# FoX prompt attention written out step by step, with projections between its steps and the past's bias summed page by page

## What is computed

```python
h = rmsnorm(x, ln_g);  z = h @ w_in          # fq fk fv ff fg | gq gk gv glr gg | ma mb
fq, fk = rmsnorm per head;  logf = log_sigmoid(ff + b)
# prompt: causal softmax(q k^T * scale + c_q - c_k) @ v with c = cumsum(logf)
# sample: the same over 32 paged blocks of 128 past tokens and the 8 new ones
lf_past = cache_logf[page_table];  c_past = cumsum(lf_past over 4096 tokens)
a = (o_fox * silu(fg)) @ w_up_a;  b = (rmsnorm(o_gla) * silu(gg)) @ w_up_b
y = x + (sigmoid(ma) * a + sigmoid(mb) * b) @ w_out
```

## Time and profile before

| | us |
|---|---|
| median of 3 runs | 1828.0 (1827.0 to 1829.68) |
| the profiled execution | 1815.63 |
| its span, first to last instruction | 1813.9 |
| PE / DVE / ACT / POOL busy | 1564.8 / 689.7 / 621.1 / 493.4 |
| mean granted TensorE clock | 0.951 of full |

### The profile page before, as it was taken

The page is one execution under the profiler, slowest core; times in us unless marked ns, Lnnn a source line. Parts: engine busy times, 40 slices in busy tenths (PEclk is TensorE's granted clock), DMA queues, the critical chain, the costliest instruction groups (busy, mean ns, idle before and its releaser), DMA issues. The chain is left out here.

```text
span 1813.9 us, 35678 instructions
## 1 busy us (share of the span) xinstructions
PE 1564.8 (86%) x11525; PEld 1304.4 (72%) x11525; DVE 689.7 (38%) x1513; ACT 621.1 (34%) x1319; POOL 493.4 (27%) x935
## 2 busy tenths in 40 slices
PE   3597979889669898899988999999987748999998
PEld 2494858778458676688766887768755548888887
DVE  5326153442643444534445344453443112333211
ACT  5135242434422434324343244442433225111111
POOL 0042332423262134233332333443140012111000
PEclk7699999999979999999999999999998879999999
DMA  4111212212055376667666666776655542322143
GB/s 130 46 47 25 81 32 60 51 53 59 14 155 168 112 225 213 208 189 211 209 201 205 198 199 203 222 228 192 200 162 165 170 179 93 141 96 85 50 117 113
DMA packets 154692, 249.72 MB, mean 138 GB/s; under 512 B 37321, under 2 KB 63434, under 8 KB 153954
## 3 DMA queue, kind: packets, MB, share of 16 engines
q1 hardware_dynamic: 122978, 215.78, 38.2%
q0 software_dynamic: 31552, 31.96, 6.6%
HBM read 217.40 MB, written 30.22 MB: 137 GB/s over the span
## 5 line engine op out<-in xcount | busy, mean ns | idle before, releaser
L280 PE MATMUL psum<-h_hi,w_hi 128*128 128x384 f32 (+1 forms) x1536 | 555.5, 362 | 62.5 <-issue 31.7
L280 PE MATMUL psum<-h_hi,w_lo 128*128 128x384 f32 (+1 forms) x1536 | 511.8, 333 | 0.0
L280 PE MATMUL psum<-h_lo,w_hi 128*128 128x384 f32 (+1 forms) x1536 | 511.3, 333 | 0.0
L280 PEld LDWEIGHTS psum<-h_hi,w_hi 128*128 128x128 f32 x1536 | 296.7, 193 | 130.2 <-issue 117.0
L1239 POOL DMA_DIRECT2D sc<-tmp_bias x512 | 252.6, 502 | 304.4 <-PE psum L1674 300.6
L280 PEld LDWEIGHTS psum<-h_lo,w_hi 128*128 128x128 f32 x1536 | 297.6, 194 | 3.0
L280 PEld LDWEIGHTS psum<-h_hi,w_lo 128*128 128x128 f32 x1536 | 296.0, 193 | 0.0
L579 POOL DMA_DIRECT2D lfk<-in_cache_logf x256 | 136.9, 535 | 259.1 <-issue 259.1
L1643 PE MATMUL psum<-con,k_page 128*128 128x128 f32 x1024 | 154.6, 277 | 32.8 <-DVE k_t L1168 22.2
L1643 PEld LDWEIGHTS psum<-con,k_page 128*128 128x128 f32 x1024 | 121.9, 142 | 53.8 <-issue 49.2
L1293 ACT ACTIVATE k_t<-psum 128x512 f32<-128x512 f32 x128 | 75.9, 593 | 201.0 <-PE psum L1643 200.8
(11 more groups left out here) (242 smaller groups left out, 2003.1 us busy)
## 6 DMA issues: line engine op xcount, KB each, us to landing
k_page<-in_cache_k SPq DMA_DIRECT2D x256, 256.0 KB, 3.5
v_page<-in_cache_v SPq DMA_DIRECT2D x256, 256.0 KB, 3.1
w_raw<-in_w_tiles SPq DMA_DIRECT2D x64, 512.0 KB, 4.6
g_pair<-tmp_gates SPq DMA_DIRECT2D x16, 544.0 KB, 4.6
sc<-tmp_bias POOLq DMA_DIRECT2D x512, 16.0 KB, 2.9
tmp_gates<-tm POOLq DMA_DIRECT2D x24, 192.0 KB, 3.5
tmp_ogla<-gate POOLq DMA_DIRECT2D x4, 1088.0 KB, 5.9
g_pair<-tmp_ogla SPq DMA_DIRECT2D x8, 544.0 KB, 4.9
```

Source lines behind the costliest of these rows:

```text
L280: m = pe.matmul(out, wt[:, s, k, :], h[:, k, t0:t0 + w], start=(k == 0 and a == 0), stop=(k == KT_ - 1 and a == 2))
```

## The change

1. `build_fox` no longer loops. `fox_order` writes one list of steps that all engines follow: the projections of pair 0 up to the first chunk of its gate tile, then the attention of pair i with the remaining gate chunks of pair i and the projections of pair i+1 between its steps. A chunk is cut into four parts of 6 matmuls. In the last pair two of the 12 merge gates that GLA projected take that place. Parts are placed in proportion to the costs in the list.
2. The ring has two banks, 0 and 1. Banks 6 and 7 take, in turn, everything else that is copied out (`lifted`): transposes, sums of squares, weighted values. A step waits until the one two places before it has been copied. `q_fm`, `k_fm`, `v_tok` and `ofox` get a second buffer.
3. The gate's sigmoid is done straight from the bank, one chunk at a time, without parking.
4. The past: a page of log forgets lands as one row of 4 KB on one partition, 128 pages in each of two groups. DVE scans the 128 tokens of each head in a page (8 scans per group), one matmul with a constant triangle (`later`) sums the later pages, and DVE subtracts. The scans of group 0 stand in DVE's list in pair 1, those of group 1 in pair 2, each after step 30 of the attention (behind t = 3's scores and before query block 1 is gated). SP stores each group in four DMAs.
5. `build_gla` has 34 projection tiles instead of 36.

```diff
-        with pe.Fori(0, NHP) as i:
...
+def projection_steps():
+    out, after = [], {}
+    tiles = fox_tiles()
...
+            if kind in (K, Q):
+                e = 3 * (kind - K) + c
+                later(n, c, FOX_PARTS - 1, (("sq", n, c), 0))
+                later(n, c + 1, 0, (("nm", i, e), 0.65), (("evac", n, c), 0))
+            else:
+                later(n, c + 1, 0, (("evac", n, c), 0))
...
+def attention_steps(i):
+    def scores(t):
+        return [(("sc", i, t), 0.28 * (t + 1) + 0.1)]
+    def soft(t, hh):
+        return [(("sm", i, t, hh), 0), (("ex", i, t, hh), 0)]
+    def turn(t, g):
+        n = min(4, t + 1 - 4 * g)
+        return [(("pt", i, t, g, hh), 0.11 * n + 0.05) for hh in range(2)]
+    out = scores(0) + soft(0, 0) + soft(0, 1)
+    for t in range(TT):
+        more = t + 1 < TT
+        if more:
+            out += scores(t + 1)
+        out += turn(t, 0)
+        if more:
+            out += soft(t + 1, 0)
+        if t >= 4:
+            out += turn(t, 1)
+        if more:
+            out += soft(t + 1, 1)
+        out.append((("inv", i, t), 0))
+        if t:
+            out.append((("pv", i, t - 1), 0.22 * t + 0.3))
...
+    for i in range(NHP):
+        k = cut(("z", 4 * i + G, 1, 0))
+        steps += [s for s, _ in proj[:k]]
+        proj = proj[k:]
+        k = cut(("z", 4 * (i + 1) + G, 0, 0)) if i < NHP - 1 else len(proj)
+        fill, proj = proj[:k], proj[k:]
+        own = attention_steps(i)
+        if i in (1, 2):
+            own = own[:30] + [(("lfscan", i - 1, h), 0) for h in range(H)] + own[30:36] + [(("lf", i - 1), 0.2)] + own[36:]
+        total, work = sum(c for _, c in fill), sum(c for _, c in own)
+        done = placed = 0.0
+        for s, cost in own:
+            steps.append(s)
+            done += cost * total / work
+            while fill and placed + fill[0][1] <= done + 0.3:
+                placed += fill[0][1]
+                steps.append(fill.pop(0)[0])
...
-        stream.phase(0, 4, (6, 0, 1))
+        stream.phase(0, 0, (0, 1))
...
+        def lift_bank(*st):
+            return bank[6 + lift_of[st][0] % 2]
+        def wait_bank(eng, *st):
+            n = lift_of[st][0]
+            if n >= 2:
+                wait_copied(eng, *lift_at[n - 2])
...
-                with pool.Fori(0, NHP) as i:
-                    W(pool, "lf_turned2", i, 2, 0)
-                    for g in range(PG):
-                        for b in range(NB):
-                            page = pool.value_load(pages[0:1, ds(i * PG + (b * NPG + g), 1)], min_val=0, max_val=NPHYS - 1)
-                            pool.dma_start(lfk[:, g, b * H:(b + 1) * H], ins["cache_logf"][ds(page, 1)]
-                                           .rearrange("o p h -> (o p) h")).then_inc(lf_in, 16)
+                for a in range(NB * NPG):
+                    page = pool.value_load(pages[0:1, a:a + 1], min_val=0, max_val=NPHYS - 1)
+                    pool.dma_start(lfp[a % P:a % P + 1, a // P, :], ins["cache_logf"][ds(page, 1)]
+                                   .rearrange("o p h -> o (p h)")).then_inc(lf_in[a // P], 16)
...
+                    if kind == G:
+                        sig = eg[:, 0:w]
+                        sigmoid_dve(dve, lambda name: W(dve, name, i, 3, c + 1), inc, zb, sig)
+                        W(dve, "g_sig", i, 3, c + 1)
...
+                        T(ofox[:, i % 2, t0:t0 + wp], zb[:, 0:wp], sig[:, 0:wp], ALU.mult).then_inc(stream.z_read, 1)
...
-                dve.tensor_tensor_scan(lfc[:], one[0:NB * H, :].to_broadcast([NB * H, PAST]), lfc[:], 0.0, ALU.mult,
-                                       ALU.add).then_inc(past_cum, 1)
...
+                def lf_scan(g, h):
+                    if h == 0:
+                        dve.wait_ge(one_set, 1)
+                        dve.wait_ge(lf_in[g], 16 * P)
+                        if g:
+                            dve.wait_ge(b_stored, 4 * 16)
+                    dve.tensor_tensor_scan(lfc[:, h, :], one[:].to_broadcast([P, PAGE]),
+                                           lfp[:, g, :].rearrange("p (t h) -> p h t", h=H)[:, h, :], 0.0, ALU.mult, ALU.add).then_inc(page_cum, 1)
+                def lf_bias(g):
+                    wait_lifted(dve, "lf", g)
+                    dve.tensor_copy(suffix[:], lift_bank("lf", g)[:, 0:H]).then_inc(lift_dve, 1)
+                    wait_copied(dve, "lf", g)
+                    T(lfc[:], suffix[:].unsqueeze(2).to_broadcast([P, H, PAGE]), lfc[:], ALU.subtract).then_inc(bias_set, 1)
...
+GATES_IN_FOX = 2
-    out, m = [], 2 * KT_ - GATES_AT_END
+    out, m = [], 2 * KT_ - GATES_AT_END - GATES_IN_FOX
-        stream.phase(TT * 2, 0, (0, 1))
+        stream.phase(4 * NHP + GATES_IN_FOX, 0, (0, 1))
```

More of the change, by code:

```diff
@@ L57 @@
 NCONST = _w
+CONST_W["later"] = (_w, 128)
 VEC_W = {}
@@ L482, in _, with fox_tiles @@
                 m.then_inc(lf_turned, 1)
[L485 to L495, removed]
+V, K, Q, G = range(4)
+FOX_PARTS = 4
+FOX_LIFTED = ("vt", "kt", "nm", "pt", "pv", "lf")
+def fox_tiles():
+    return [(n, i) for i in range(NHP) for n in (V, K, Q, G)] + [("m", x) for x in range(GATES_IN_FOX)]
@@ new lines, in projection_steps, with later @@
+def projection_steps():
+    out, after = [], {}
+    tiles = fox_tiles()
+    def later(n, c, part, *steps):
+        at = 3 * n + c
+        after.setdefault((at // 3, at % 3, part), []).extend(steps)
+    for n, (kind, i) in enumerate(tiles):
+        for c in range(3):
+            if kind in (K, Q):
[4 more added lines that the diff above has]
+                later(n, c + 1, 0, (("evac", n, c), 0))
+        for p in range(3):
+            if kind == V:
+                later(n, 3, p + 1, (("vt", i, p), 0.45))
+            if kind == K:
+                later(n, 4, p + 1, (("kt", i, p), 0.45))
+    for n in range(len(tiles)):
+        for c in range(3):
+            for part in range(FOX_PARTS):
+                out.append((("z", n, c, part), 1.05))
+                out += after.pop((n, c, part), [])
+    for key in sorted(after):
+        out += after[key]
+    return out
@@ new lines, in fox_order, with cut @@
+def fox_order():
+    proj = projection_steps()
+    steps = [("cbc", 0)]
+    def cut(step):
+        return next((k for k, (s, _) in enumerate(proj) if s == step), len(proj))
+    for i in range(NHP):
[15 more added lines that the diff above has]
+                steps.append(fill.pop(0)[0])
+        steps += [s for s, _ in fill]
+        steps.append(("end", i))
+    return steps
@@ L569, in _ @@
+                run(sp, {"cbc": bias_rows, "z": z, "vt": v_store, "kt": k_store, "lf": bias_store, "end": end})
+                for s in range(2):
+                    sp.wait_ge(of_stored[s], NHP // 2 * 16)
+                sp.wait_ge(v_stored, NHP * 32)
+                sp.wait_ge(k_stored, NHP * 32)
+                sp.wait_ge(b_stored, 8 * 16)
             @block.gpsimd
@@ new lines, in square @@
+                def square(n, c):
+                    kind, i = tiles[n]
+                    e = 3 * (kind - K) + c
+                    w = CHUNKS[c][1]
+                    act.wait_ge(stream.projected, stream.chunk(0, n, c))
+                    if e >= 2:
+                        wait_lifted(act, "nm", i, e - 2)
+                    elif i:
+                        wait_lifted(act, "nm", i - 1, e + 4)
+                    inc(act.activation(sq[:, e % 2, 0:w], stream.bank_of(n, c), ACT.Square), "squared")
@@ L790, in turn_kv @@
[L790 to L800 removed]
+                opened(pe, lifted, S["s_mm"], S["pv_mm"])
@@ L829, in weigh @@
-                def weigh(i, t):
-                    W(pe, "pt0", i, NG, group(t, t // 4) + 1)
-                    W(pe, "pt1", i, NG, group(t, t // 4) + 1)
-                    W(pe, "o_gated", i, TT, t)
-                    if t == 0:
-                        pe.wait_ge(stream.z_read, stream.chunk(i, G, 2))
+                        for hh, head in enumerate(heads):
+                            m = pe.matmul(bank[2 + 2 * hh + c // 4][:, 0:n], q_fm[head, i % 2, t * P:(t + 1) * P],
+                                          k_fm[head, i % 2, c * P:c * P + n], start=True, stop=True)
@@ L896 @@
+                run(pe, {"z": z, "vt": v_turn, "kt": k_turn, "nm": norm_sum, "sc": scores, "pt": turn_prob, "pv": weigh, "lf": page_suffix})
 PARTS = 4
```

563 lines of the change are left out of this document (267 added, 296 removed).

## The result

| | before | after |
|---|---|---|
| median of 20 runs of each, us | 1822.33 | 1834.82 |
| ratio, 95% interval | | 1.0058, 1.0042 to 1.0075 |
| the profiled execution, its span | 1815.6, 1813.9 | 1832.1, 1830.4 |
| first matmul of GLA | 515.56 | 558.46 |
| first matmul of the merge | 1476.4 | 1492.88 |

The change makes the kernel slower by 0.6%. 1860 was predicted, within 1800 to 1880: the direction came out, but the loss was 12.5 us by the medians where 32 were forecast. By stages, in the two traces: FoX ends 42.9 us later, GLA takes 26.4 us less, and the merge is the same, +16.5 us.

A forecast was written before the change was run, and what follows sets the result against it. PE was taken as the bound, with idle time in FoX's attention and end; a 52 us page wait starts GLA 52 us later, less 20 in GLA is +32 us, put on the median: 1860, range 1800 to 1880.

The forecast's parts named there:

- PE released from the page wait: FoX, third pair: PE idles 52 us, from 358 to 410, while DVE waits for pages until 405, then scans and gates.
- from there to FoX's last matmul: FoX after the page wait: 131 us of list, 2.5 us for the low clock, 1 + 13 us of waits.
- to GLA's first: End of FoX: last gate chunk's sigmoid, its store and the barrier take some 10 us without matmuls, against 22.3.
- The cadence of the pages: POOL's log-forget page loads: 1.30 - 0.046 = 1.25 us each, all landed at 405; bounds 1.10 and 1.32.
- fewer descriptors should not help: POOL's page loads: one row instead of 128 saves nothing, since the load's 0.534 us is not in the issue chain.
- the half us before a load: POOL's page loads: the 0.54 us between the move and the load's start stays when the loop is written out.
- The first rival: POOL: the half us goes with the loop's computed addresses, pages land at 223, 26.5 us won, 1801; chance 0.20.
- DVE's arrival: FoX, pair 2: DVE reaches the scans of group 1 at 83.8 + 237.2 + 27 + 3 = 351, before the pages.
- The ruler: FoX: one us of the new list's costs is about one us of PE; a tile is 11.8 us, two 23.7.
- before the release nothing on PE matters: FoX ahead of the page wait's end: time won on PE there only lengthens the wait.
- The last pair: FoX, last attention: 13 us of idle time, against 9 per other pair, with half as much to put between.
- What is taken out there is worth nothing: GLA's last 92 us wait for value pages, so two tiles fewer (23.7 us) give 20 us, between 10 and 24.

## Why the prediction was right and wrong

The mechanism was right: DVE's wait for the pages, 40.7 us, fell within the 40 to 65 I had given, and PE's gap lay at 349.0 to 389.6 where I had said 358 to 410. Three sizes were off, and the largest two, of opposite sign, cancelled in part. That cancelling was luck: had the stretch behind the release been as long as forecast, the sum would have been near +4 instead of +16.5.

| term | predicted | measured | |
|---|---|---|---|
| PE released from the page wait | 410 | 389.6 | -20.4 |
| from there to FoX's last matmul | 131 + 2.5 + 14 = 147.5 | 160.1 | +12.6 |
| to GLA's first | 10 | 8.7 | -1.3 |
| GLA | -20 | -26.4 | -6.4 |
| sum against before | +32 | +16.5 | -15.5 |

**The cadence of the pages** is the step that failed: I put a page at 1.25 us, and it took 1.176, which over 255 pages is 19 us of the 20.4 in the first row. My step was "Written out, the index needs no 0.046 us; the rest stays". In steady state it fell from 1.217 (148.16, 149.38, 150.60, 151.81 in the timeline of before) to 1.121. Putting the 128 rows back gave 1.135, so 0.014 of the 0.096 are the shorter load and 0.08 the loop's index, of which I had read off only the one instruction with a row of its own. The rest are pauses, in which loads stop for 0.3 to 3 us: 1.30 - 1.22 = 0.08 a load in the loop, 1.176 - 1.12 = 0.056 written out; I had carried the loop's over. Ten of the 21 in the kernel after are reads of a page number that take 0.5 to 1.4 us instead of 0.285, and they make up 6.5 of the 14.2 us; the 256 loads from fixed addresses, without reads, paused once, for 3.2 us. What causes them was not tried. My bounds were 1.10 and 1.32, and I took a value in the upper half because of the pauses. That "fewer descriptors should not help" held but for the 0.014, and that the half us before a load stays was right. The first rival, built on the half us going, needed 1.04 or less, and at 1.12 it could not happen. The row I held against it, SP's 1.10 in GLA, is of loads of the same kind: SP too reads a page number before each (L1185). The Trainium skill's page "DMA: Bandwidth & Descriptors", section "Anatomy of one DMA — SWDGE (gpsimd) path", says that completion and not setup is most of a load's fixed cost. The trace of the fixed pages agrees in this: a load every 0.476 us, landing 1.9 us after its issue. The some 50 ns that it gives for the dispatch are not what paces this stream. With the page number read for each load, the trace of the change shows 1.12 us, and that decided.

**DVE's arrival** was forecast at 351 and was 343.8. The ruler held: two tiles in FoX move GLA's start by 521.27 - 497.65 = 23.6 us against 23.7. That it is so close is luck: the last pair itself grew by 26.2, the wait ahead of GLA by 2.0, and what lies before the last pair, with the same list, was 4.6 shorter in that trace. The idle time of an equal pair was 13.1, 8.4 and (with the scans in pair 3) 11.5 us beyond the list's 87.3, for which I had said 9. The list starts 5 us ahead of where I put it: the first scores come at 127.3, not 83.8 + 48.6. This error cost nothing, as the forecast said it would ("before the release nothing on PE matters"), and the run with the sigmoid in steps and the scans in pair 2 shows that.

**The last pair** was my worst estimate of a stall: 13 us, and it was 88.1 - 64.1 = 24. I named what stands in DVE's list ("some 3.2 us during which DVE's list stands") and counted it once per query block at small t, as in the other pairs; in the last pair it comes for the pair's own gate chunks and then for those of two more tiles, seven times with a wait of DVE. Taking those round trips apart gave 8.2 us back there; how the rest divides stays open.

**GLA** gave 26.4 for two tiles, not 20. "What is taken out there is worth nothing" was drawn from the right rows and applied wrongly: no tile was taken out of the last 92 us, where PE still issues 588 matmuls against 594. PE's busy time in GLA fell by 23 us, 864.7 to 841.6. The remaining 3 us, and why the next two tiles give only 18.6, are open.

The rest of the distance between 1860 and 1834.8 is no term of the sum: the kernel before ran at 1822.3 here, 5.7 below the median I had added to, and the medians lie 12.5 apart where the profiled executions lie 16.4 apart.

## What to carry to other kernels

When work is moved from the end of a stage into an engine's in-order list, compute two clock times, when the engine gets there and when the data does, and put it behind the later one; here one pair later is worth 2% of the kernel. Write multi-engine round trips into the lists as separate steps, with other work between, rather than as one step. And before tuning the part ahead of a fixed-time wait, remove the wait: until then a gain there is invisible.

## Hardware behaviour I had not expected

- A page load on POOL from a fixed address starts every 0.476 us. From an address in a register the step is 0.577, 0.10 of it register work and a move, and the read of the page number from SBUF takes another 0.546 (load 0.285, register work 0.152 and 0.018, and gaps). A read did not overlap an issue, one by one or in fours: 1.12 us a page.
- 128 rows of 32 bytes instead of one row of 4 KB add 0.05 us to a load's time on POOL and 0.014 to the cadence.
- After the gap of 40.6 us the first projection matmuls of the kernel after are 0.32 us apart (390.04, 390.36, 390.68) where they were 0.17 before it (347.56, 347.73, 347.91): 1.2 instead of 2.4 GHz. The granted clock in the gap reads 0.54, and full speed is back at 393.9. The same half-speed matmuls open GLA, until 564.6, after 8.7 us without matmuls. From 389.6 to 393.9 at half speed some 2 us were lost, near the 2.5 of the forecast, so this gap cost a little more than its length.
